# An attention block in two-part FP32: another order at its entry and end, one rope on VectorE, one power for a double norm

## The reference, cut to what matters

```
x = x + 0.5 * swiglu(rmsnorm(x, norm_ffn2), ...)      # first block, matrix "d1"
x = rmsnorm(x, norm_final)                             # new residual
h = rmsnorm_2(x, norm1_g) * (1.0 + sc1) + sh1          # second block
qkv = h @ w_qkv                                        # 16 query heads, 2 key and value heads of 64
q = partial_rope(rmsnorm_2(q, q_gain), positions)      # norm of each head, 16 of its 64 columns turned
k = partial_rope(rmsnorm_2(k, k_gain), positions)
p = softmax([q k^T * scale inside a window of 128, sink])
x = x + g1 * ((p @ v) @ w_o)                           # "wo_a"
h = rmsnorm_2(x, norm2_g) * (1.0 + sc2) + sh2          # then swiglu: "gu2", ...
```

## Time and profile before

| | us |
|---|---|
| median of three runs | 1181.45 (1181.1 to 1182.91) |
| the profiled execution | 1182.49 |
| its span | 1180.7 |
| TensorE, products | 1150.6 busy |
| VectorE | 847.4 busy |
| ScalarE | 651.8 busy |
| GpSimd | 69.4 busy |

### The profile page before, as it was taken

One profiled execution on the slowest core, in us unless ns is written; L12 is line 12 of the kernel. 1 busy time (PEld: TensorE's weight loads), 2 busy tenths in 40 slices (PEclk: granted clock), 3 DMA queues, 4 the chain that ended last, 5 costly groups with the idle time before them and its releaser, 6 DMA issues.

```text
span 1180.7 us, 16925 instructions
## 1 busy us (share of the span) xinstructions
PE 1150.6 (97%) x6646; PEld 986.6 (84%) x6646; DVE 847.4 (72%) x1328; ACT 651.8 (55%) x1084; POOL 69.4 (6%) x85
## 2 busy tenths in 40 slices
PE   6999999999999999999989989999999999999998
PEld 5888888899999888888865678888888988888887
DVE  6788976545447779988667577888777757677654
ACT  6554555466556565555467455555545775655551
POOL 0000000000002000500223010000020001000000
PEclk9999999999999999999999989999999999999999
DMA  9786884754444589998442247888738533677640
GB/s 336 267 286 240 341 282 150 283 198 164 149 157 143 183 320 320 365 341 310 143 147 96 67 167 269 294 301 318 271 138 309 197 108 111 225 245 250 241 159 36
DMA packets 42382, 263.50 MB, mean 223 GB/s; under 512 B 7360, under 2 KB 7744, under 8 KB 12480
## 3 DMA queue, kind: packets, MB, share of 16 engines
q1 hardware_dynamic: 42304, 262.42, 62.5%
HBM read 261.31 MB, written 1.10 MB: 222 GB/s over the span
## 4 chain that ended last, share of the span: by engine, by line
PE 86%; DVE 5%; issue 4%; ACT 3%; POOL 2%; DMA 1%; SPq 0%; POOLq 0%; DVEq 0%; ACTq 0%
PE ps L351 83%; DVE wl L1023 2%; PE ps L540 1%; ACT wh L1589 1%; PE ps L953 1%; DMA raw<-in_stream 1%; PE ps L720 1%; DVE xn L1128 0%; DVE x L1058 0%; ACT arena L1840 0%; POOL arena L2037 0%; POOL small L1972 0%; POOL res L1978 0%; POOL xn L2020 0%; DVE xn L1070 0%
## 5 line engine op out<-in xcount | busy, mean ns | idle before, releaser
L1023 DVE TENSOR_TENSOR wl<-raw,wh 128x1024 fp32r<-128x1024 f32 x374 | 450.3, 1225 | 38.6 <-ACT wh L1589 37.8
L351 PE MATMUL ps<-x,wh 128*128 128x512 f32 (+1 forms) x1984 | 445.3, 347 | 0.0
L1589 ACT ACTIVATE wh<-raw 128x1024 fp32r<-128x1024 f32 x374 | 388.6, 1051 | 45.8 <-PE ps L351 30.5
L351 PEld LDWEIGHTS ps<-x,wh 128*128 128x128 f32 x1984 | 342.4, 190 | 45.1 <-issue 3.4
L351 PE MATMUL ps<-x,wl 128*128 128x256 f32 x1568 | 264.7, 282 | 0.0
L351 PEld LDWEIGHTS ps<-x,wl 128*128 128x128 f32 x1568 | 236.7, 191 | 11.3
L351 PE MATMUL ps<-wh,x 128*128 128x512 f32 (+1 forms) x600 | 185.9, 386 | 2.9 <-DVE x L1058 2.3
L351 PE MATMUL ps<-wh,hh 128*128 128x512 f32 x404 | 160.5, 397 | 1.4 <-ACT arena L1895 1.4
L351 PE MATMUL ps<-wl,hh 128*128 128x512 f32 x404 | 158.4, 392 | 0.0
L351 PE MATMUL ps<-wh,hl 128*128 128x512 f32 x404 | 157.8, 391 | 0.0
L351 PEld LDWEIGHTS ps<-wh,x 128*128 128x128 f32 x600 | 112.2, 191 | 26.3 <-issue 3.3
(11 more groups left out here) (182 smaller groups left out, 839.1 us busy)
## 6 DMA issues: line engine op xcount, KB each, us to landing
raw<-in_stream SPq DMA_DIRECT2D x233, 1024.0 KB, 5.1
arena<-vectors SPq DMA_DIRECT2D x12, 512.0 KB, 6.0
arena<-in_tables SPq DMA_DIRECT2D x7, 576.0 KB, 6.3
raw<-in_stream SPq DMA_DIRECT2D x4, 512.0 KB, 8.5
gain_sb<-in_gains SPq DMA_DIRECT2D x3, 512.0 KB, 8.2
res<-in_x SPq DMA_DIRECT2D x4, 256.0 KB, 5.1
gain_sb<-in_c SPq DMA_DIRECT2D x2, 512.0 KB, 6.7
out_dram<-res SPq DMA_DIRECT2D x3, 256.0 KB, 2.0
```

Source lines behind the costliest of these rows:

```text
L351: return e.matmul(o, a, b, start=start, stop=stop)
L1023: e.tensor_tensor(WL[:, n % NW, :], src, WH[:, n % NW, :].bitcast(F32), ALU.subtract).then_inc(*w_lo.tick(n))
L1589: e.activation(WH[:, m % NW, :], src, ACT.Copy).then_inc(*w_hi.tick(m))
```

## The change

- The double norm: instead of two factors in turn, `(sum of squares with gain) + D*EPS*(mean square)` is formed in two small steps and raised to -0.5 once. The power for the new residual comes behind it. The product with the final gain for token half 0, column half 1, goes from GpSimd to VectorE.
- TensorE at the entry: transposes of half 1 behind query unit 1, the quarter behind unit 2; the turns of keys and of the first queries go in between query units of half 1; the second turn goes from step 2 to step 1.
- VectorE at the entry: one low half instead of three ahead of the transposed rows; sums for both key halves before either is turned; the second keys behind the sum of the first queries.
- ScalarE at the entry: one high half fewer ahead of the keys and values of half 0; table load and one high half ahead of those of half 1; in the loop one high half from step 1 to 2.
- The rope of step 5 is VectorE's.
- The end: VectorE's and ScalarE's part of `boundary(4)` for half 0 is woven into steps 17 and 18 and around the last weighting; the weight splitting that stood ahead of the boundary comes behind it.

```diff
@@ TensorE
-                pe.wait_ge(*(pooled if t else vec).of("turned", t, 8 * c))
+                pe.wait_ge(*(pooled if (t, c) == (1, 1) else vec).of("turned", t, 8 * c))
...
             quarter(0)
-            for k in range(4):
+            for k in range(2):
                 for c in range(2):
                     queries(k, 0, c)
             for half in range(2):
                 transposed(final_rows(q, 1)[half], vec.of("out", q, 1, half), 6 + half, "x", q, 1, half)
                 evicted[6 + half] = [x_lo.of("x", q, 1, half)]
+            for c in range(2):
+                queries(2, 0, c)
             quarter(1)
-            for ks in ((4, 5), (6, 7)):
+            for k in range(3, 6):
                 for c in range(2):
-                    for k in ks:
-                        queries(k, 0, c)
+                    queries(k, 0, c)
+            for c in range(2):
+                for k in range(6, KT):
+                    queries(k, 0, c)
             for k in range(4):
                 for c in range(2):
+                    if (k, c) == (2, 0):
+                        turn_k()
+                    if (k, c) == (3, 1):
+                        turn_q(0, 0, 6)
                     queries(k, 1, c)
-            turn_k()
-            turn_q(0, 0, 6)
...
-                if i in (2, 7, 11):
-                    turn_q(*{2: (0, 1, 7), 7: (1, 0, 0), 11: (1, 1, 7)}[i])
+                if i in (1, 7, 11):
+                    turn_q(*{1: (0, 1, 7), 7: (1, 0, 0), 11: (1, 1, 7)}[i])
@@ VectorE
+            if (q, t) == (4, 0):
+                dv.wait_ge(*formed.of("values", "w", 12 + c))
...
+        def product(t, c):
...
+            e.tensor_tensor(XN[t][c], RES[t][c], GAIN[1][c], ALU.mult).then_inc(*vec.tick(("product", t, c)))
...
             if q == 3:
+                dv.wait_ge(*vec.of("msq", q, t))
+                dv.wait_ge(*acted.of("final square", t, 0))
+                e.scalar_tensor_tensor(msf[t][:, 0:1], msq[t], float(D * EPS), ssf[t][:, 0:1], ALU.mult, ALU.add).then_inc(
+                    *vec.tick(("msf", t)))
                 dv.wait_ge(*acted.of("final square", t, 1))
-                e.tensor_tensor(msf[t][:, 0:1], ssf[t][:, 0:1], ssf[t][:, 1:2], ALU.add).then_inc(*vec.tick(("msf", t)))
                 dv.wait_ge(*vec.of("msf", t))
-                dv.wait_ge(*pooled.of("power", q, t))
-                e.tensor_scalar(msf[t][:, 1:2], msf[t][:, 0:1], rstd[t][:, 1:2], float(D * EPS), ALU.mult, ALU.add).then_inc(
-                    *vec.tick(("final msq", t)))
-                if meanwhile:
-                    low_to(meanwhile[1])
+                e.tensor_tensor(msf[t][:, 1:2], msf[t][:, 0:1], ssf[t][:, 1:2], ALU.add).then_inc(*vec.tick(("final msq", t)))
                 dv.wait_ge(*pooled.of("final power", t))
-                e.tensor_tensor(msf[t][:, 0:1], rstd[t][:, 2:3], rstd[t][:, 0:1], ALU.mult).then_inc(*vec.tick(("factor", t)))
-                dv.wait_ge(*vec.of("factor", t))
...
-            low_to(n + 6)
+            low_to(n + 4)
             x_low(q, 1)
-            low_to(n + 7)
-            keys_turned(0)
             low_to(n + 9)
-            keys_turned(1)
+            scales(0, 16, 2, QK[0][:, 1024:1152])
+            scales(1, 16, 2, QK[1][:, 1024:1152])
+            turned_heads(0, 16, 2, bank(place["quarter", 3, 0], P), True)
             scales(0, 0, 8, XN[0][0])
+            turned_heads(1, 16, 2, bank(place["quarter", 3, 1], P), True)
             scales(0, 8, 8, XN[0][1])
...
-                    turned_heads(1, 2 * i - 10, 8, bank(2 + i // 8), False)
+                    turned_heads(1, 2 * i - 10, 8, bank(2 + i // 8), i == 5)
...
+                if i == 17:
+                    residual(4, 0, 0, "wo_a")
+                if i == 18:
+                    gained(4, 0, 0)
+            n = N["tm", "wo_a", KT - 1]
             weighted(3)
+            residual(4, 0, 1, "wo_a")
+            gained(4, 0, 1)
             y_low(3)
-            n = N["tm", "wo_a", KT - 1]
-            at(n, n - TAIL + NW)
-            boundary(4, "wo_a", n)
+            mean_square(4, 0)
+            normalised(4, 0)
+            low_to(n + 4)
+            residual(4, 1, 0, "wo_a")
+            x_low(4, 0)
+            gained(4, 1, 0)
+            residual(4, 1, 1, "wo_a")
+            gained(4, 1, 1)
+            mean_square(4, 1)
+            low_to(n + 5)
+            normalised(4, 1)
@@ ScalarE
-            high_to(n + 7)
+            high_to(n + 6)
...
             keys_values(0)
             x_high(q, 1)
+            high_to(n + 7)
+            e.preload_act_table_set("natural_log_exp_and_others")
+            high_to(n + 8)
             keys_values(1)
-            e.preload_act_table_set("natural_log_exp_and_others")
             high_to(n + 9)
...
+                if i == 18:
+                    square(4, 0, 0)
             y_high(3)
+            square(4, 0, 1)
             n = N["tm", "wo_a", KT - 1]
-            at(n, n - TAIL + NW)
-            boundary(4, n)
+            high_to(n + 4)
+            x_high(4, 0)
+            square(4, 1, 0)
+            square(4, 1, 1)
+            high_to(n + 5)
@@ GpSimd
+            if q == 3:
+                po.wait_ge(*vec.of("final msq", t))
+                e.tensor_tensor(rstd[t][:, 2:3], msf[t][:, 1:2], mhalf[:, 0:1], ALU.pow).then_inc(*pooled.tick(("final power", t)))
             po.wait_ge(*vec.of("msq", q, t))
...
         for t in range(2):
-            for c in range(2):
+            for c in range(1 + t):
```

More of the change, by code:

```diff
@@ L1102, in mean_square, with normalised @@
                 *vec.tick(("msq", q, t)))
-        def normalised(q, t, meanwhile=()):
-            if meanwhile:
-                low_to(meanwhile[0])
+        def product(t, c):
+            dv.wait_ge(*acted.of("final gain"))
+            dv.wait_ge(*formed.of("rows", 1, t))
+            dv.wait_ge(*vec.of("sum", 3, t, c))
+            e.tensor_tensor(XN[t][c], RES[t][c], GAIN[1][c], ALU.mult).then_inc(*vec.tick(("product", t, c)))
+        def normalised(q, t, meanwhile=None):
+            if meanwhile is not None:
+                low_to(meanwhile)
             if q == 3:
+                dv.wait_ge(*vec.of("msq", q, t))
+                dv.wait_ge(*acted.of("final square", t, 0))
+                e.scalar_tensor_tensor(msf[t][:, 0:1], msq[t], float(D * EPS), ssf[t][:, 0:1], ALU.mult, ALU.add).then_inc(
+                    *vec.tick(("msf", t)))
                 dv.wait_ge(*acted.of("final square", t, 1))
-                e.tensor_tensor(msf[t][:, 0:1], ssf[t][:, 0:1], ssf[t][:, 1:2], ALU.add).then_inc(*vec.tick(("msf", t)))
                 dv.wait_ge(*vec.of("msf", t))
-                dv.wait_ge(*pooled.of("power", q, t))
-                e.tensor_scalar(msf[t][:, 1:2], msf[t][:, 0:1], rstd[t][:, 1:2], float(D * EPS), ALU.mult, ALU.add).then_inc(
-                    *vec.tick(("final msq", t)))
-                if meanwhile:
-                    low_to(meanwhile[1])
+                e.tensor_tensor(msf[t][:, 1:2], msf[t][:, 0:1], ssf[t][:, 1:2], ALU.add).then_inc(*vec.tick(("final msq", t)))
                 dv.wait_ge(*pooled.of("final power", t))
-                e.tensor_tensor(msf[t][:, 0:1], rstd[t][:, 2:3], rstd[t][:, 0:1], ALU.mult).then_inc(*vec.tick(("factor", t)))
-                dv.wait_ge(*vec.of("factor", t))
             else:
                 dv.wait_ge(*pooled.of("power", q, t))
-            factor = msf[t][:, 0:1] if q == 3 else rstd[t][:, 0:1]
+            factor = rstd[t][:, 2:3] if q == 3 else rstd[t][:, 0:1]
             for c in range(2):
@@ L1136, in boundary @@
                 residual(q, 0, c, name)
+                if (q, c) == (3, 1):
+                    product(0, c)
                 gained(q, 0, c)
@@ L1399, in turned_heads @@
                 dv.wait_ge(*vec.of("turned", t, h0))
-            def keys_turned(t):
-                scales(t, 16, 2, QK[t][:, 1024:1152])
-                turned_heads(t, 16, 2, bank(place["quarter", 3, t], P), True)
-            low_to(n + 6)
+            low_to(n + 4)
             x_low(q, 1)
-            low_to(n + 7)
-            keys_turned(0)
             low_to(n + 9)
-            keys_turned(1)
+            scales(0, 16, 2, QK[0][:, 1024:1152])
+            scales(1, 16, 2, QK[1][:, 1024:1152])
+            turned_heads(0, 16, 2, bank(place["quarter", 3, 0], P), True)
             scales(0, 0, 8, XN[0][0])
+            turned_heads(1, 16, 2, bank(place["quarter", 3, 1], P), True)
             scales(0, 8, 8, XN[0][1])
@@ L1614, in square @@
             if q == 3:
-                ac.wait_ge(*pooled.of("product", t, c))
+                ac.wait_ge(*(vec if (t, c) == (0, 1) else pooled).of("product", t, c))
                 ac.wait_ge(*acted.of("square", q, t, c))
@@ L1963, in power @@
                 po.wait_ge(*pooled.of("constants"))
-            if q == 3:
-                e.tensor_tensor(rstd[t][:, 0:2], msq[t].to_broadcast([P, 2]), mhalf[:, 14:16], ALU.pow).then_inc(
```

(15 more changed lines are left out.)

13 lines of the change are left out of this document (6 added, 7 removed).

## The result

The changed kernel takes 1170.3 us, the median of four runs (1169.88 to 1170.83), where the kernel before, four runs beside it, has 1181.28 (1180.18 to 1182.91). The ratio is 0.9906, with a 95% interval of 0.9889 to 0.9923. Forecast was 1170.0. TensorE is still the bound.

A forecast was written before the change was run, and what follows sets the result against it. TensorE, busy 97% of the span, was taken as the bound. Gains of 5.7 (A) + 0 (B) + 5.7 (C) = 11.4 us from the median 1181.45 gave 1170.0 us, range 1167 to 1176.

The forecast's parts named there:

- A: Entry, up to the score loop: turned orders and the single power gain 5.7 us, from 4 to 6.5.
- B: Score loop: 0.8 us gained at the bank, 0.8 lost by VectorE's rope; sum 0, from -1.5 to +1.5.
- The bank's 0.8: Score loop: turning the second queries one step earlier frees their bank, gaining 0.8 us with the restart.
- The step that left the clock's loss where it was: Score loop: new waits together no shorter than the old, so the 1.5 us lost at the lower clock stays.
- C: Attention's end: 8.4 us of wait, restart and slow clock less 2.7 newly late, 5.7 gained, from 3.5 to 7.5.
- The term of 3.0 us at half clock: Attention's end: behind the 5.14 us wait TensorE runs 6.1 us at half clock, 3.0 us lost.
- The term of 2.7 us for what is late next: Attention's end: new waits of 0.3 on x's low parts and 1.85 on half 1's rows, with two restarts 2.7 us.
- (1): Loop and end: new waits drop TensorE to half clock, some 3 us less gained, 1173 us; chance 0.18.
- (2): Entry and end: a chain runs late because GpSimd shares VectorE's time, gain 6 to 7 us, 1175; chance 0.15.
- (3): Score loop: its waits hidden and the clock kept, better at 1167.5 us; chance 0.10.
- (4): Start of the FFN: the new order moves the stalls there one for one, no gain, 1181 us; chance 0.04.
- (5): Score loop: VectorE becomes its bound and delays every later step, slower at 1182 to 1185 us; chance 0.03.

The follow-up runs named there:

- rope_back: The changed kernel with only the rope of loop step 5 back on GpSimd: 1169.05 us, ratio to the kernel before 0.9902.
- turns_back: The changed kernel with keys and queries turned behind the queries and the second turn in step 2, as before: 1171.26 us, ratio 0.9904.
- end_back: The changed kernel with the attention's end alone ordered as before: 1176.74 us, ratio to the kernel before 0.9964.
- power_back: The changed kernel with the double norm's two powers in turn as before, VectorE's product kept: 1172.14 us, ratio 0.9912.
- better: The changed kernel with VectorE's rope split over steps 5 and 6, step 6's low half in 7, ScalarE's last high half one square earlier: 1169.57 us, 0.9894.
- fill: The kernel before with 20 unread products where TensorE waits 5.14 us before the transposes at the attention's end: 1180.69 us, ratio 0.9995.
- best: rope_back with ScalarE's last high half ahead of both squares and the scaled rows ahead of VectorE's split: 1168.74 us, ratio 0.9894.
- better_pool: rope_back with ScalarE's last high half ahead of its last square: 1169.16 us, ratio to the kernel before 0.9888.

## Why the prediction was right, point by point

**The bound.** Right: TensorE's waits and its clock were all that moved; VectorE's busy time is the same to 0.3 us, and from the first product behind the last transposes on nothing gives the gain back (the tail from there is 485.72 us before and 485.79 after).

**A, 5.7 predicted, 5.99 measured.** The score loop starts 27.60 us behind the FFN's mark, predicted 27.9. VectorE and GpSimd at the double norm in after, timeline:

```profile
580.49 0.69 DVE L1072 SCALAR_TENSOR_TENSOR res<-ps,res 128x512 f32<-128x512 f32 x1 [1.98 <-PE ps L351]
581.21 0.69 DVE L1117 TENSOR_TENSOR xn<-res,gain_sb 128x512 f32<-128x512 f32 x1
...
583.17 0.57 POOL L1998 TENSOR_TENSOR small<-small 128x1 f32<-128x1 f32 x1 [3.52 <-DVE small L1131]
583.77 1.42 DVE L1141 SCALAR_TENSOR_TENSOR arena<-arena,small 128x512 f32<-128x512 f32 x2 [0.68 <-POOL small L1998]
...
592.26 0.55 POOL L1998 TENSOR_TENSOR small<-small 128x1 f32<-128x1 f32 x1 [1.50 <-DVE small L1131]
592.85 1.41 DVE L1141 SCALAR_TENSOR_TENSOR arena<-arena,small 128x512 f32<-128x512 f32 x2 [0.66 <-POOL small L1998]
```

The scaled rows start 3.28 us behind the mark, 4.61 before (rows 5): 1.33 earlier, predicted 1.3. Those of half 1 start 12.36 behind it, 15.16 before (rows 6): 2.8 earlier, predicted 2.9. The choice of 0.55 for the power beside an idle VectorE, and not rows 6's 1.45, carried this: 0.57 and 0.55. Of the three small waits foreseen, that on a low half came (0.24 instead of 0.3), that on ScalarE's copy of the turned queries was 0.09 instead of 0.2, and that before the second transposes did not come, which with its restart is the 0.3.

**B, 0 predicted; +0.35 or -0.6 measured.** The rope's wait changed its name as predicted, to VectorE's maxima before pair 7 and ScalarE's copy before pair 8. The waits are shorter than worked out: none before pair 6, 0.59 instead of 1.2, 1.26 instead of 1.6, but 0.48 more before pair 10, which I had not seen: 2.3 us where 3.4 stood. The sum had also left out their restarts, some 0.8 us for three by its own 0.26, so the two errors offset each other: by rope_back the rope costs 1.1 where 0.8 stood. The bank's 0.8 was not kept beside VectorE's rope, as turns_back shows, and about 0.5 of it without. 0.5 less 1.1 is the -0.6 against the executions of before whose clock stayed in the loop; the execution shown lost 1.0 by the clock on top, which gives the +0.35. The step that left the clock's loss where it was is wrong: in none of the six profiles with the new waits (after twice, end_back, power_back, turns_back, better) did the clock fall in the loop. But behind the old wait it fell in only two of eight, so it is not shown that the new waits are what keeps it. B came out near nothing by errors of up to 1 us of both signs, which is chance.

**C, 5.7 predicted; 6.9 against the execution that the prediction was made from, 5.5 against the others.** The mechanism is right: the 5.14 us are gone (no wait at all there), the clock is 1.00, and a wait before the transposes of half 1 is new. Two terms are mis-sized and offset each other. The term of 3.0 us at half clock: 2.35 at most and 1.0 in the other executions. I had taken half of the 6.1 us as lost. Timeline of TensorE in before, then in its second execution, behind the same wait:

```profile
686.58 0.63 PE L351 MATMUL ps<-wh,hh 128*128 128x512 f32 x1
687.00 0.63 PE L351 MATMUL ps<-wl,hh 128*128 128x512 f32 x1
```
```profile
686.85 0.39 PE L351 MATMUL ps<-wl,hh 128*128 128x512 f32 x1
687.07 0.39 PE L351 MATMUL ps<-wh,hl 128*128 128x512 f32 x1
```

At the lower level products start 0.43 us apart instead of 0.23, in before up to 689.56, in the second execution only up to 686.56. And the eight transposes with the restart take 1.62 us to the next product, where fill has 1.08, so they do not double. That makes 2.56 us against fill up to the eleventh product, and fill loses 0.2 of it again further on. The term of 2.7 us for what is late next: 0.70 and a restart, about 1.0. The timeline of after shows why:

```profile
661.39 0.68 DVE L1078 TENSOR_TENSOR xn<-ps,arena 128x512 f32<-128x512 f32 x1
...
668.28 1.41 DVE L1141 SCALAR_TENSOR_TENSOR xn<-xn,small,arena 128x512 f32<-128x512 f32 x2 [0.67 <-POOL small L2004]
...
673.12 1.03 PE L540 MATMUL ps<-ident,xn 128*128 128x128 f32 x8
...
680.00 1.23 DVE L1029 TENSOR_TENSOR wl<-raw,wh 128x1024 fp32r<-128x1024 f32 x1 [0.73 <-ACT wh L1616]
...
681.94 1.32 PE L540 MATMUL ps<-ident,xn 128*128 128x128 f32 x8 [0.70 <-DVE xn L1141]
```

From the first gated product to the first scaled rows it takes 6.9 us, not the 8.4 that I had laid end to end. Up to the end of the outputs' last low half it is 6.1 us, as worked out. Behind it 0.8 are left and not 2.3, because ScalarE's square of column half 1 (666.19 to 666.91 with its read) runs beside VectorE's gain step and that low half and not behind them. So the rows have 4.8 us of cover and not 3.2. For half 1 about 0.5 of these 1.6 us are lost again where VectorE stands 0.73 for a high half that ScalarE does behind two squares, and that is what best takes away. The low parts of x were no wait.

**The sum.** The forecast gain was 11.4 us, and the medians give 11.0. But it was worked out from an execution of before whose clock fell both in the loop and longer at the end, and against that one the gain is 13.1: C is 1.2 above its forecast, A and B 0.3 each. The median of before lies between the two kinds of execution, and that the number of the median was hit so closely is luck; that the two large parts, entry and end, bring some 6 and 5.5 to 6.9 us is not.

**The rivals.** (1), the clock at the new waits: none, in no window of after. What the Trainium skill tells of short idle spells between groups of products (TensorE: Matmul & The Clock Gate, "A second HAM failure mode: psum-queue depth-cycling"), of a bf16 kernel there, did not happen here: the waits of 0.59, 1.26, 0.48 and 0.33 us in a row left the clock at 1.00. (2), chains late by GpSimd: not in after, but the mechanism is real, as power_back (1.69 us for the first power of half 1) and better_pool (1.47) show. (3), 1167.5: the kernel best comes near it, at 1168.7, though not by hiding the waits of B. (4): only the 0.70 before the transposes of half 1. (5): no sign; the loop up to pair 8 is 18.07 us, not above the 18.41 of before.

## What to carry to other kernels

Read for each chain how long its last input has been lying there: half of this gain came from a norm that could start ten microseconds earlier (its first gated product stands 11.7 us ahead of TensorE's arrival instead of 1.4), and had stood behind splits that waited for someone else. A wait taken from one engine's order comes back in another's unless that engine has room at just this step, as the rope did. And price a fall of the clock from more than one execution of the same kernel.

## What the runs showed of the hardware

- Of three profiles of one kernel, with the same waits at the same places, the clock fell behind a wait of 1.34 us in one; with five more that have this wait, in two of eight. Behind 5.14 us it fell in all four profiles that have this wait (three of before, end_back), for 1.0 to 2.35 us of lost time by the execution.
- A power of 128 x 1 on GpSimd takes 0.55 to 0.57 us beside an idle VectorE and 1.47 beside VectorE's two-input split. The Trainium skill, GPSIMD Engine Reference, section "Specifications", says that GpSimd shares its memory interfaces with VectorE and contends with VectorE's instructions of two inputs there; the trace agrees, and the price is 0.9 us for an operation on a single column.
- The start of a launch scatters by 1.7 us (first product at 12.69 to 14.35 in fourteen profiles), which is more than several of the edits studied here are worth.
